# Second block of a two-block model: where the merges and the splits of the output weights stand in the engines' queues

## The reference

```python
proj = rmsnorm(h, norm1_g) @ w_in
q, k, v, xr, gr, g_merge = jnp.split(proj, splits, axis=-1)
attn = bidirectional_gqa(q, k, v)
xc = centred_dwconv(xr, conv_w, conv_b)
rnn = (rg_lru(xc, ..., False) + rg_lru(xc, ..., True)) * jax.nn.gelu(gr)
g_attn, g_rnn = jnp.split(sigmoid(g_merge), 2, axis=-1)
mix = g_attn * attn + g_rnn * rnn          # "merge"
h = h + mix @ w_out
hn = rmsnorm(h, norm2_g)
g, u = jnp.split(hn @ w_ffn_in, 2, axis=-1)
h = h + (silu(g) * u) @ w_ffn_out

def rg_lru(xc, wa, ba, wx, bx, lam, reverse):   # for each of 8 blocks of 128 columns
    r = sigmoid(xc @ wa + ba); i = sigmoid(xc @ wx + bx)
    a = exp(8 * r * log_sigmoid(lam))
    return scan(a, sqrt(1 - a * a) * i * xc)    # forwards, and backwards in the second direction
```

## Time and profile before

| | |
|---|---|
| runs, us | 2319.83, 2322.12, 2328.80 (median 2322.12) |
| the profiled execution | 2322.02 us, its span 2320.2 us |
| busy over the span | PE 89%, DVE 41%, ACT 27%, POOL 20% |
| mean granted clock of PE | 0.944 of full |
| recurrence with its granules | 1774 to 1895 us |
| output projection | 1895 to 1939 us |
| from there to the feed-forward | 1939 to 1953 us |

### The profile page before, as it was taken

One profiled execution on the slowest core, in us unless ns is written; L12 is line 12 of the kernel. 1 busy time (PEld: TensorE's weight loads), 2 busy tenths in 40 slices (PEclk: granted clock), 3 DMA queues, 4 the chain that ended last, 5 costly groups with the idle time before them and its releaser, 6 DMA issues.

```text
span 2320.2 us, 24316 instructions
## 1 busy us (share of the span) xinstructions
PE 2067.3 (89%) x10160; PEld 1519.7 (65%) x10160; DVE 960.5 (41%) x1371; ACT 637.1 (27%) x960; POOL 469.8 (20%) x319
## 2 busy tenths in 40 slices
PE   5999898999998979888788879888787878999999
PEld 4879787888887763333333337667665666888787
DVE  6864454432333561111111126754544794222343
ACT  3442332321323201000000014343134753222221
POOL 4532132232322511111111020211002240000021
PEclk8899899999999979999899989999999999999999
DMA  4661231221324368999999964201111133323220
GB/s 154 214 175 52 55 89 39 37 73 37 73 37 148 132 239 318 409 411 403 411 412 406 422 271 162 73 22 61 46 46 46 37 109 109 109 73 109 73 91 37
DMA packets 97514, 360.77 MB, mean 155 GB/s; under 512 B 9834, under 2 KB 34572, under 8 KB 85112
## 3 DMA queue, kind: packets, MB, share of 16 engines
q1 hardware_dynamic: 81856, 330.50, 39.6%
q0 software_dynamic: 8240, 19.00, 2.4%
q10 hardware_dynamic: 7304, 9.66, 1.3%
HBM read 338.41 MB, written 29.10 MB: 158 GB/s over the span
## 4 chain that ended last, share of the span: by engine, by line
PE 75%; DVE 12%; ACT 5%; issue 5%; POOL 1%; ACTq 1%; DMA 1%; PEld 0%; SPq 0%; PEldq 0%; DVEq 0%; POOLq 0%
PE ps L269 72%; PE ps L273 3%; DVE H L259 1%; ACT ST L265 1%; ACT L265 1%; DVE ST L253 1%; DVE BG L253 1%; ACT M L266 1%; DVE sm L2894 1%; DVE WL L253 1%; ACT M L265 1%; DVE M L256 1%; POOL WL L253 1%; DVE M L253 0%; DVE ST L2816 0%
## 5 line engine op out<-in xcount | busy, mean ns | idle before, releaser
L269 PE MATMUL ps<-W,BG 128*64 128x512 f32 x672 | 202.6, 647 | 34.6 <-issue 34.6
L269 PE MATMUL ps<-XH,WS 128*128 128x512 f32 x704 | 217.7, 390 | 0.0
L269 PE MATMUL ps<-HTH,WL 128*128 128x512 f32 x448 | 183.1, 409 | 0.0
L269 PEld LDWEIGHTS ps<-ST 128*128 128x128 f32 x1376 | 168.9, 193 | 8.8 <-POOL ST L253 1.7
L269 PE MATMUL ps<-ST 128*128 128x64 f32 (+1 forms) x1376 | 169.0, 275 | 1.2 <-POOL ST L253 1.0
L269 PEld LDWEIGHTS ps<-XH,WS 128*128 128x128 f32 x704 | 132.8, 189 | 27.7
L2094 DVE COPY BG<-ps 128x512 f32<-128x512 f32 x32 | 22.1, 691 | 298.4 <-PE ps L269 298.4
L269 PE MATMUL ps<-XL,WS 128*128 128x512 f32 x352 | 137.6, 391 | 7.7 <-DVE XL L253 7.7
L269 PEld LDWEIGHTS ps<-W,BG 128*64 128x64 f32 x672 | 62.6, 148 | 124.6 <-issue 123.4
L263 ACT ACTIVATE BG<-ps 128x512 f32<-128x512 f32 x48 | 28.5, 595 | 379.2 <-PE ps L273 346.4
L269 PE MATMUL ps<-X2H,GV 128*128 128x512 f32 (+1 forms) x512 | 131.5, 348 | 0.0
(11 more groups left out here) (386 smaller groups left out, 4389.3 us busy)
## 6 DMA issues: line engine op xcount, KB each, us to landing
W<-in_w SPq DMA_DIRECT2D x42, 2048.0 KB, 27.3
W<-in_w_in SPq DMA_DIRECT2D x27, 2048.0 KB, 14.0
ST<-in_w SPq DMA_DIRECT2D x14, 2048.0 KB, 26.2
U<-in_w SPq DMA_DIRECT2D x14, 2048.0 KB, 26.6
M<-in_w SPq DMA_DIRECT2D x13, 2048.0 KB, 27.2
HT<-in_w SPq DMA_DIRECT2D x13, 2048.0 KB, 27.4
W<-in_w_ffn_in SPq DMA_DIRECT2D x22, 1024.0 KB, 7.6
ypad<-BG SPq DMA_DIRECT2D x23, 512.0 KB, 15.0
```

Source lines behind the costliest of these rows:

```text
L269: return p.e.matmul(o, lhsT=l, rhs=r, start=start, stop=stop, skip_group_check=True)
```

## The change

On DVE the merges go out of their places and are collected in a list `due`; they are issued behind the `q` steps of every odd unit (so merges 0, 1 behind q3, merges 2, 3 behind q5, merges 4, 5 behind q7) and the rest, 6 and 7, at the end. ACT's four sigmoids of unit n wait for the scans of unit n-2 (`scan_done`), and only its exponentials for `rfin_done`. DVE splits three pieces of half 0 behind granule s7 (`v_wo_first`); the other 13 pieces (order `WO_PARTS`) are copied by ACT, three ahead of the last gate sigmoid and ten behind it, and subtracted by DVE: three ahead of the u step of unit 6, three ahead of that of unit 7, three at the end, and after merges 6 and 7 the last four. POOL has no part in them. In the stage after, ACT does the scaling (`s_normed3`), DVE only the reciprocal, and the first split of the feed-forward weights goes to the front of both queues.

```diff
-        def v_wo2(k0, k1):
+        WO_PARTS = [(1, 0), (1, 1), (1, 2), (0, 3), (0, 4), (0, 5), (1, 3), (1, 4), (1, 5), (0, 6), (0, 7), (1, 6), (1, 7)]
+        def v_wo_first():
             v.wait_ge(*w_ready[N_OUT])
             v.wait_ge(*B["rg", 7, 3].full())
-            for k in range(k0, k1):
+            for k in range(3):
...
+        def s_wo_high(i, j):
+            for y, k in WO_PARTS[i:j]:
+                s.wait_ge(*w_ready[N_OUT + y])
+                s.wait_ge(*B["s", 7].full())
+                act(WOH[y][:, k, :], weights3(N_OUT + y)[:, k, :], ACT.Copy).then_inc(wo_hi)
+        def v_wo_low(i, j):
+            for n in range(i, j):
+                y, k = WO_PARTS[n]
+                v.wait_ge(wo_hi, n + 1)
+                tt(v, WOL[y][:, k, :], weights3(N_OUT + y)[:, k, :], WOH[y][:, k, :].bitcast(F32), SUB).then_inc(wo_lo[y])
...
 s_second, kind "s":
+                    if n == 7:
+                        s_wo_high(0, 3)
                     act(s_tmp[n % 2], t.at, ACT.Sigmoid).then_inc(t.drained)
 v_second:
+                if j == len(GRAN) - 2:
+                    v_wo_first()
                 elif kind == "s":
-                    if n == 5:
-                        v_wo2(0, 5)
                     f.mul_s[n] = True
                     if f.mul_r[n]:
-                        v_merge2(n)
+                        f.due.append(n)
 s_rnn:
             if n > 1:
-                s.wait_ge(rfin_done, n - 1)
+                s.wait_ge(scan_done, 2 * n - 2)
...
             s.wait_ge(c8_done, 1)
+            if n > 1:
+                s.wait_ge(rfin_done, n - 1)
 v_rnn:
+            if n % 2:
+                v_merges(f)
             yield
             yield
+            if n > 5:
+                v_wo_low(3 * (n - 6), 3 * (n - 5))
...
             tt(v, Vr[:, n, :], Vr[:, n, :], z, MUL).then_inc(rfin_done)
             if f.mul_s[n]:
-                v_merge2(n)
+                f.due.append(n)
 v_middle, at its end:
+            v_wo_low(6, 9)
+            v_merges(f)
+            v_wo_low(9, 13)
 v_out:
-            v_wo2(5, 8)
+            v_split_in(0)
             v_added(0)
             v_added(1)
-            v_normed(0)
+            v_rms3(0)
...
 s_out:
-            s_wo2()
+            s_wo_high(3, 13)
             s.wait_ge(mx_done, 8)
+            s_split_in(0)
             s_squared(0)
             s_squared(1)
+            s_normed3(0)
             s_squared(2)
+            s_normed3(1)
             s_turn3(0)
             s_squared(3)
+            s_normed3(2)
+            s_normed3(3)
             s_turn3(1)
-            s_split_in(0)
             s_turn3(2)
             s_turn3(3)
+        def s_normed3(m):
+            s.wait_ge(n2_inv, m + 1)
+            act(XN[:, m, :], H[:, m, :], ACT.Copy, scale=ssr[:, m:m + 1]).then_inc(n2_done)
 queue of POOL:
             g_middle()
-            g_wo2()
             g_ffn_out()
```

More of the change, by code:

```diff
@@ L1972, in build @@
         c_m, c_rp = sem("meta_loaded"), sem("rope_loaded")
-        alpha_done, msq_done, mnorm_done, meta_done = sem("alpha_h"), sem("meta_rms"), sem("meta_normed"), sem("meta_turned")
+        alpha_done, msq_done, mnorm_done = sem("alpha_h"), sem("meta_rms"), sem("meta_normed")
         rows3 = [(c_row[0], 80), (c_row[1], 64)]
@@ L2480, in __init__ @@
                 self.mul_s, self.mul_r = [False] * 8, [False] * 8
+                self.due = []
         GRAN = [("v", 0), ("k", 0), ("k", 1)] + [("q", n) for n in range(8)] + [("a", n) for n in range(8)] + \
@@ L2560, in build @@
         s_tmp = [Sf[:, 1064 + 512 * j:1576 + 512 * j] for j in range(2)]
-        vs_done, xr_done, mx_done, rfin_done = sem("gated_rnn"), sem("x_conv"), sem("mix"), sem("rnn_out")
+        vs_done, mx_done, rfin_done = sem("gated_rnn"), sem("mix"), sem("rnn_out")
         def wide(t):
@@ L2692, in build @@
         WOL = [cols8(WL[slot[N_SEC + 11 + y]]) for y in range(2)]
-        wo_hi, wo_lo = sem("w_out_high"), [sem("w_out_low_dve"), sem("w_out_low_pool")]
-        def v_wo2(k0, k1):
+        wo_hi, wo_lo = sem("w_out_high"), [sem("w_out_low_first"), sem("w_out_low_second")]
+        WO_PARTS = [(1, 0), (1, 1), (1, 2), (0, 3), (0, 4), (0, 5), (1, 3), (1, 4), (1, 5), (0, 6), (0, 7), (1, 6), (1, 7)]
+        def v_wo_first():
             v.wait_ge(*w_ready[N_OUT])
             v.wait_ge(*B["rg", 7, 3].full())
-            for k in range(k0, k1):
+            for k in range(3):
                 raw, hi = weights3(N_OUT)[:, k, :], WOH[0][:, k, :]
@@ L2944, in build @@
         c16 = neg
-        c_g, c8_done = sem("rg_weights"), sem("lambda")
+        c_g, c8_done, scan_done = sem("rg_weights"), sem("lambda"), sem("scans")
         def attended(E):
@@ L3028, in g_rnn, with v_merges @@
             f.mul_r[n] = True
+        def v_merges(f):
+            for m in f.due:
+                v_merge2(m)
+            f.due = []
         def v_rnn(n, f):
@@ L3049, in v_rnn @@
                 if dr == 0:
-                    v.e.tensor_tensor_scan(th, rr, ii, 0.0, MUL, ADD).then_inc(v.up())
+                    v.e.tensor_tensor_scan(th, rr, ii, 0.0, MUL, ADD).then_inc(scan_done)
                 else:
-                    v.e.tensor_tensor_scan(th[:, ::-1], rr[:, ::-1], ii[:, ::-1], 0.0, MUL, ADD).then_inc(v.up())
-            here = v.now
+                    v.e.tensor_tensor_scan(th[:, ::-1], rr[:, ::-1], ii[:, ::-1], 0.0, MUL, ADD).then_inc(scan_done)
+            here = scan_done, 2 * n + 2
             while f.out <= at_gran["r", n]:
@@ L3117, in build @@
         XL = alias("XL", "ST", 10 * 512, [P, 8, T])
-        n2_rms, n2_done = sem("n2_rms"), sem("n2_normed")
+        n2_rms, n2_inv, n2_done = sem("n2_rms"), sem("n2_inverse"), sem("n2_normed")
         x3_hi, x3_lo = sem("x3_high"), sem("x3_low")
@@ L3166, in v_added, with v_rms3 @@
                 tt(v, o, o, t.at, ADD).then_inc(t.drained)
-        def v_normed(m):
+        def v_rms3(m):
             v.wait_ge(n2_rms, m + 1)
-            v.e.reciprocal(ssr[:, m:m + 1], ssr[:, m:m + 1]).then_inc(v.up())
-            v.wait_ge(*v.now)
-            ts(v, XN[:, m, :], H[:, m, :], ssr[:, m:m + 1], None, MUL, None).then_inc(n2_done)
+            v.e.reciprocal(ssr[:, m:m + 1], ssr[:, m:m + 1]).then_inc(n2_inv)
         def v_out():
-            v_wo2(5, 8)
+            v_split_in(0)
             v_added(0)
             v_added(1)
-            v_normed(0)
+            v_rms3(0)
             v_added(2)
-            v_normed(1)
+            v_rms3(1)
             v_gain3(0)
             v_added(3)
-            v_normed(2)
+            v_rms3(2)
             v_low3(0)
             v_gain3(1)
-            v_normed(3)
+            v_rms3(3)
             v_low3(1)
             v_gain3(2)
-            v_split_in(0)
+            v_gain3(3)
             v_low3(2)
-            v_gain3(3)
             v_low3(3)
```

## The result

The changed kernel took 2302.06 to 2309.07 us in four runs (median 2306.14), the one before 2319.83 to 2328.80 (median 2323.89). The ratio is 0.9926, interval 0.9908 to 0.9944: 17 us less, between 13 and 21. A second job, with six runs of the changed kernel and eleven of the one before, gave 0.9924 (0.9906 to 0.9941). The prediction was 2307.

What follows compares the result with a forecast made beforehand. PE, with 75% of the chain, bounds the kernel, some 30 us of its idle time within reach; 3.2 + 2.4 + 2.6 + 6.7 + 0.4 = 15.3 off 2322.02 gives 2306.7, stated as 2307, range 2300 to 2317.

Steps and rivals of the forecast that it cites:

- Round 1: Recurrence round with pairs 2,3 entering, 31.91 us before: sigmoids of unit 2 start at end of scans 0, -3.2 us.
- A: Moment in a round at which PE goes on with a granule after the pair's gates; 1806.01 before, 1802.8 forecast.
- Round 2: Recurrence round with pairs 4,5 entering, 33.12 us before: -2.4 us despite a 4.6 us PE gap at r6.
- B: End of the q steps in a round, A + 13.26; A to B left alone, B to next A changed.
- Round 3: Recurrence round with pairs 6,7 entering, 33.45 us before: -2.6 us, 0.8 from half clock and 1.8 from B to A.
- Last round: Last round up to the projection, 22.05 us before: the 6.11 gap at s7 and 1.5 half clock go, -6.7 us.
- The projection: Output projection, 44.64 us of PE without a gap: 0 change if weights and banks are ready before PE needs them.
- Behind it: Stretch from projection to feed-forward, 13.62 us before: split and scalings leave DVE, scaling on ACT costs; -0.4 us, within 1.5.
- Rival 1: The rounds give nothing, as longer PE gaps and half clock eat the earlier sigmoids' gain: 2315 us; chance 0.17.
- rival 2: The rounds give more, with no half clock and no slow scans: 2302 us; chance 0.16.
- Rival 3: Bank 1 late in the projection because ACT's sigmoid of s7 stands behind three copies: 2311 to 2313 us; chance 0.1.
- Rival 4: Slower than before: DVE's long instructions have another cause than POOL; 2342 us with all 41 slow; chance 0.07.

Runs made afterwards that it cites:

- d_scale_dve: Changed kernel with the scaling of the row tiles behind the output projection back on DVE; projection start to feed-forward 55.39 us against 57.57.
- e: Changed kernel with the output weights split as before, five pieces on DVE between granules s6 and s7; last round 20.75 us against 15.34.
- run c: Changed kernel with merges 0 to 4 moved ahead of granules r5, s4 and s7; rounds 2 and 3 30.79 and 28.57 us, median 2301.84, ratio 0.9918.
- a: Changed kernel with merges in their old places and sigmoids waiting for rfin_done again; rounds 31.93, 33.12, 33.46 us, last round 21.19.
- run j: Changed kernel with eight instead of three weight copies by ACT ahead of the sigmoid of s7; projection start to feed-forward 59.04 us against 57.57.
- run f: Changed kernel with the eight subtractions of half 1 back on POOL; projection start to feed-forward 63.58 us against 57.57.

## Why the prediction was right, point by point

**Round 1, -3.2; measured -2.8.** The sigmoids of unit 2 started 21.0 us into the round, as stated. The end of scans 1 decided A, and A came 2.1 us behind it and not 1.6. The missing 0.4 is PE at half clock behind a gap of 2.19 (four gate matmuls 1.91 at 1796.25; 1.16 for the same ones in the kernel d_scale_dve, whose round took 28.55).

**Round 2, -2.4; measured -1.5.** From B (1811.22 + 0.71) to the next A 17.27, forecast 17.5, with the gap of 4.48 (4.6) ended by granule r6. The way from A to B, called untouched, took 14.35 instead of 13.26, by the half clock with which the round began. That the other way met its forecast is luck. In runs d and e round 1 ended without half clock; there A to B took 13.25, as forecast, and B to A 18.7, though the gap was the same (4.49 and 4.50), and the round came out at 31.94 and 31.92. Run d, from the end of the gap to A:

```profile
1820.59:1833.79 13.20, 12.85 (x44) 10.30 (x45) 12.96 (x14) 7.64 (x11) 3.56 (x3) 0.77 0.00 0
```

PE was busy for 12.85 there, for 11.42 in the same stretch of the changed kernel (granted clock 0.87), and for 10.34 in run c (1.00). So the term that was sized too small is the half clock: 1.5 counted for the round, 2.2 (1.1 in front of the gap and 1.1 behind it) in the changed kernel, 2.5 in run d. The mechanism was right: A follows the last scan by 3.02 and not by 1.6, so PE's gates are what is late.

**Round 3, -2.6; measured -3.3.** From A to B 13.26, all of the half clock gone and not half of it; from B to A 16.89, forecast 16.9, but not for the reason given. The prediction kept POOL's work and the scans apart; its 16.9 lay between 16.2 without and 17.3 with half clock. In the trace PE is not late (A follows the last scan by 1.59), and one scan took 2.28 beside a gate product of POOL, one fence each:

```profile
1850.35 2.28 DVE L3071 TENSOR_TENSOR_SCAN ST<-ST 128x528 f32<-128x528 f32 x1
```

```profile
1849.94 1.57 POOL L253 TENSOR_TENSOR BG<-BG,ST 128x512 f32<-128x512 f32 x1 [17.48 <-ACT ST L265]
```

The gap in front of s5 was 2.97 and not 4.6, since PE came to it 1.3 late through granule r7, slowed by POOL (1.81 and 2.23 for its copy and subtraction, 0.69 and 1.23 in the granules beside it).

**Last round, -6.7; measured -6.7** (15.34 against the 15.3 from A to the projection's start, with 1.10 for bank 0). The mechanism was incomplete: the gap was put down to five pieces and merge 5 together, as work. Runs a and e show that each of the two alone makes most of the gap, and that merge 5 waits for POOL's product for s5. That wait could have been found in the trace of before (POOL at 1876.45); the change took both away, so the number came out all the same.

**The projection, 0 if its cover holds; it held.** Bank 1 had the 1.4 us of margin that was forecast (run j), DVE's last date was 1903 for a forecast of A + 43.3 = 1902.7, and PE had no gap until the first transposed tile.

**Behind it, -0.4; projection and this stage together measured -0.7.** Two larger terms nearly cancel inside: +2.2 for the scaling on ACT and -2.9 for the rest of the new order (run d), of which 0.7 comes from the gain of tile 3, which the prediction doesn't price. That the net is so near is in part luck.

**Sum: -15.3 forecast, -15.0 in the lengths, -17 in the runs' ratio.** The parts miss by +0.4, +0.9, -0.7, 0.0 and -0.3 and cancel to 0.3. The median of 2306.14 lies nearer to 2307 than the working deserves: the starting point, 2322.02, was 1.9 below the median of before (2323.89), and the medians differ by 17.8, some 3 more than the stages gave. Rival 1 (rounds give nothing) is out: they gave 7.6. Of rival 2, run c shows that 2.4 more were to be had. Rival 3 needs 1.4 us of delay on ACT (run j) and did not come. Rival 4's condition, long DVE instructions without POOL, is refuted by run f.

## What to carry to other kernels

When an edit takes work from in front of a waiting instruction, look for the wait that the work was hiding: of two causes that cover each other, each taken away alone is worth little (0.9 and 1.3 us here), both together 6.7. Place deferrable work where its engine already waits for the bound engine (here ahead of r5, DVE idle for 3.07 us at 1801.85), not merely behind the critical result, and count what is queued behind it. And for a wait on a whole chain of results, check which buffer is reused at all: one line that let the sigmoids wait for the scans alone was worth about 3 of the 15 us.

## What the runs showed of the hardware

A gap of PE can be paid again as slow matmuls. Behind 4.48 us idle the matmuls of the changed kernel ran at 1.2 GHz for some 3 us (1817.43 to 1820.5), behind 4.49 in run d for over 5 (all 12 of the half granule, 0.44 each); behind 2.98 us (run f) 13 of them took 0.44 each, granted clock 0.50. By these rows the page TensorE: Matmul & The Clock Gate (section HAM oscillation) of the Trainium skill holds: PE loses its clock in an idle time and starts the next burst slowly.

The length of the gap alone doesn't tell whether it happens. Behind 2.19 us it did in the changed kernel (four gate matmuls 1.91) and behind 2.18 it didn't in run d (1.16), at the same place; behind 2.10 us transposed tile 3 took 1.97 in run d and 1.09 in the kernel before. Two gaps of one trace, the kernel before:

```profile
1798.17 2.09 PE L269 MATMUL ps<-H,BG 128*128 128x264 f32 x5 [3.02 <-ACT ST L265]
...
1864.74 1.16 PE L269 MATMUL ps<-H,BG 128*128 128x264 f32 x4 [3.05 <-ACT ST L265]
```

From 1800 to 1802, behind the first, the granted clock is 0.50; from 1864 to 1868, behind the second, it is 1.00, and the second trace of before has the same pair. What decides is open here; a forecast of such a gap needs a range and not a value.

A scan on DVE nearly doubles its length beside POOL as well (1.26 to 2.25 in run c, 2.28 in round 3 of the changed kernel), not only the copies and subtractions.
